# Comparison numbers in PSUM, spreads in three banks beside 45 downs, and paired heads in the mixer

## What is computed

```python
# first block, two layers: neighbourhood attention of 256 latents over themselves and 256 context
# keys (8 heads of 64), and in the first layer attention of the context over itself
s = einsum('q,k', q, k) * 64 ** -0.5 + bias
p = softmax(s);  o = p @ v

# second block: retrieval of 16 x 8 experts of 16384 for each token
q = (h @ w_q).reshape(B, TB, 8, 2, 128)
s = einsum('btphd,phnd->btphn', q, subkeys)
v, i = top_k(s, 16)
cand = v[..., 0, :, None] + v[..., 1, None, :]          # 256 candidates of a token and head
cidx = i[..., 0, :, None] * 128 + i[..., 1, None, :]
tv, tj = top_k(cand, 16);  eidx = take_along_axis(cidx, tj);  w = softmax(tv)
a = gelu(einsum('btd,btpkd->btpk', h, w_down[eidx]))
out = einsum('btpk,btpkd->btd', w * a, w_up[eidx])
```

## Time and profile before

| what | us |
|---|---|
| median of 3 runs | 3045.37 |
| lowest, highest | 3043.37, 3047.05 |
| profiled execution, device time | 3047.02 |
| its span from first to last instruction | 3045.2 |
| busy: PE, PEld | 2862.2 (94%), 2391.7 (79%) |
| busy: DVE, ACT, POOL | 2171.0 (71%), 1225.8 (40%), 534.0 (18%) |
| mixer's scores to pooled products, layer 0 | 562.9 to 644.6 |
| the same, layer 1 | 1549.4 to 1602.5 |
| downs of the retrieval | from about 2146 |
| first product of `Experts` on PE | 2415.4 |

### The profile page before, as it was taken

How to read it: one execution, slowest core, us unless ns; L and a number is a source line. 1 busy time by engine, 2 the same in 40 slices (tenths; PEclk the granted TensorE clock), 3 DMA queues, 4 the chain that set the end, 5 groups by cost and what they waited for, 6 DMA issues and landing times. The chain is left out here.

```text
span 3045.2 us, 40386 instructions
## 1 busy us (share of the span) xinstructions
PE 2862.2 (94%) x15682; PEld 2391.7 (79%) x15682; DVE 2171.0 (71%) x3813; ACT 1225.8 (40%) x2228; POOL 534.0 (18%) x403
## 2 busy tenths in 40 slices
PE   7999999999999999999899999389977899999997
PEld 4888878568888778888859999259967788888886
DVE  2999994558998975657656665446997777777776
ACT  2322243453222342223445455245544444444444
POOL 1111115000111110001400000003899600000000
PEclk9999999999999999999999999689999999999999
DMA  6445542123545454444414555304633356555553
GB/s 237 179 174 193 187 151 90 49 92 137 180 176 197 152 191 163 156 147 160 144 42 140 185 188 168 114 1 140 189 107 100 97 189 192 193 190 189 195 190 118
DMA packets 121295, 463.05 MB, mean 152 GB/s; under 512 B 13456, under 2 KB 26128, under 8 KB 107792
## 3 DMA queue, kind: packets, MB, share of 16 engines
q1 hardware_dynamic: 107280, 359.79, 35.9%
q0 software_dynamic: 13824, 100.67, 8.5%
HBM read 453.20 MB, written 7.21 MB: 151 GB/s over the span
## 5 line engine op out<-in xcount | busy, mean ns | idle before, releaser
L174 ACT ACTIVATE weight_hi<-weight_ring 128x512 fp32r<-128x512 f32 x1272 | 798.6, 631 | 1197.5 <-PE bank L264 1196.0
L181 DVE TENSOR_TENSOR weight_lo<-weight_ring,weight_hi 128x512 fp32r<-128x512 f32 x1154 | 868.7, 756 | 466.8 <-ACT weight_hi L174 465.1
L262 PE MATMUL bank<-operand_hi,weight_hi 128*128 128x256 f32 (+1 forms) x3168 | 1046.7, 330 | 28.5 <-DVE operand_lo L601 13.0
L263 PE MATMUL bank<-operand_lo,weight_hi 128*128 128x256 f32 (+1 forms) x3168 | 1036.8, 327 | 0.0
L264 PE MATMUL bank<-operand_hi,weight_lo 128*128 128x256 f32 (+1 forms) x3168 | 1036.1, 327 | 0.0
L262 PEld LDWEIGHTS bank<-operand_hi,weight_hi 128*128 128x128 f32 x3168 | 606.2, 191 | 95.7 <-issue 21.4
L263 PEld LDWEIGHTS bank<-operand_lo,weight_hi 128*128 128x128 f32 x3168 | 606.3, 191 | 52.7
L264 PEld LDWEIGHTS bank<-operand_hi,weight_lo 128*128 128x128 f32 x3168 | 606.0, 191 | 50.4
L859 DVE SCALAR_TENSOR_TENSOR extension_ffn<-extension_ffn,silu_c 128x512 f32<-128x512 f32 x532 | 388.0, 776 | 1.7
L262 PE MATMUL bank<-hidden_hi_ffn,weight_hi 128*128 128x512 f32 (+1 forms) x704 | 256.6, 364 | 4.0 <-DVE arena L1104 4.0
L263 PE MATMUL bank<-hidden_lo_ffn,weight_hi 128*128 128x512 f32 (+1 forms) x704 | 255.3, 363 | 0.0
(11 more groups left out here) (259 smaller groups left out, 2807.6 us busy)
## 6 DMA issues: line engine op xcount, KB each, us to landing
weight_ring<-in_ffn SPq DMA_DIRECT2D x272, 512.0 KB, 3.5
weight_ring<-in_experts SPq DMA_DIRECT2D x256, 512.0 KB, 3.5
extension_ffn<-in_w_mods POOLq DMA_DIRECT2D x96, 1024.0 KB, 7.6
weight_ring<-in_w_mix SPq DMA_DIRECT2D x56, 512.0 KB, 3.4
weight_ring<-in_w_second SPq DMA_DIRECT2D x52, 512.0 KB, 4.0
spill<-early_retrieve SPq DMA_DIRECT2D x47, 128.0 KB, 3.8
arena<-spill SPq DMA_DIRECT2D x47, 128.0 KB, 3.5
extension_mixer<-in_rel_bias SPq DMA_DIRECT2D x2, 1536.0 KB, 6.7
```

Of the source, the lines that this page charges most:

```text
L174: nc.scalar.activation(self.hi[:, g % 2, h], self.ring[:, g % NS, h], ACT.Copy).then_inc(self.rounded, 1)
L181: self.nc.vector.tensor_tensor(self.lo[:, g % 2, h], self.ring[:, g % NS, h], self.hi[:, g % 2, h].bitcast(F32), ALU.subtract).then_inc(se ...
L262: nc.tensor.matmul(out, a_hi, b_hi, start=start and n == 0, stop=False)
L263: nc.tensor.matmul(out, a_hi, b_lo, start=False, stop=False)
```

## The change

**The numbers of the comparison.** ACT copies `iota` (128x128) from SBUF into PSUM bank 7 once, among the query units. The 64 comparisons (now L2189) and the 4 large comparisons of `decode` (now L2247) read it there. Spreads therefore go round three banks, 4 to 6, and a spread waits for the copy of the batch three before it, not four.

**Counts.** K0 goes from 47 to 45 and ALONE from 22 to 20, so that the spreads begin two downs earlier and two more downs stand in `Experts`. HAND_OVER follows (43). `pairs` of the second half is cut in two parts of four heads, and `weights` of the first half stands between them.

**The mixer.** Items run by pairs of heads: for a tile of queries the even head, then the odd one. Scores of both heads are issued in a row, into two of four banks (0, 1, 6, 7), four items ahead and more. The values of a pair (four items) go into one bank, 64 partitions for each head, in four parts of one tile of keys for both heads; one part follows each transposition of a later item. ACT moves a pair's product in one instruction of 128 partitions, and `pt` is twice as large.

```diff
@@
-A_POOL = A_PT + 2048
+A_POOL = A_PT + 4096
@@
-        self.items = [(g, h, qt) for g in range(ng) for h in range(NA_H) for qt in range(2)]
+        self.items = [(g, 2 * hp + j, qt) for g in range(ng) for hp in range(NA_H // 2) for qt in range(2) for j in range(2)]
@@
+    def score_bank(self, w):
+        return (0, 1, 6, 7)[w % 4]
+
+    def turned_probs(self, n, j, kt):
+
+        return self.pt[:, 4 * (n % 2) + kt, :].rearrange("p (j q) -> p j q", j=2)[:, j, :]
@@
-        def scores(w):
-            g, h, qt = items[w]
-            lo, hi = keys(g)
-            po, q0 = 64 * (h % 2), g * S + qt * P
-            if w >= 2:
-                pe.wait_ge(self.scores_read.sem, self.scores_read.at(w - 1))
-            nc.tensor.matmul(chip.bank[w % 2][:, 0:hi - lo], u[po:po + 64, CH_Q + h // 2, q0:q0 + P],
-                             u[po:po + 64, CH_K + h // 2, lo:hi], start=True, stop=True)\
-                .then_inc(self.scored.sem, 1)
+        def scores(n):
+            if n >= 2:
+                pe.wait_ge(self.scores_read.sem, self.scores_read.at(2 * n - 2))
+            for w in (2 * n, 2 * n + 1):
+                g, h, qt = items[w]
+                lo, hi = keys(g)
+                po, q0 = 64 * (h % 2), g * S + qt * P
+                nc.tensor.matmul(chip.bank[self.score_bank(w)][:, 0:hi - lo], u[po:po + 64, CH_Q + h // 2, q0:q0 + P],
+                                 u[po:po + 64, CH_K + h // 2, lo:hi], start=True, stop=True)\
+                    .then_inc(self.scored.sem, 1)
@@
+            if part == 0:
+                pe.wait_ge(self.copied.sem, self.copied.at(4 * n + 4))
+                if n >= 2:
+                    pe.wait_ge(self.moved.sem, self.moved.at(n - 1))
+            for j in range(2):
+                h = items[4 * n + j][1]
+                mm = nc.tensor.matmul(chip.bank[4 + n % 2][64 * j:64 * j + 64, 0:S],
+                                      v[:, part + 4 - nkt, h * DH:(h + 1) * DH], self.turned_probs(n, j, part),
+                                      start=(part == 0), stop=(part == nkt - 1))
@@
         for w in range(len(items)):
-            if w + 3 < len(items):
-                scores(w + 3)
+            if w % 2 == 0 and w // 2 + 2 < len(items) // 2:
+                scores(w // 2 + 2)
             transposes(w)
-            if w >= 2 and w % 2 == 0:
-                values(w // 2 - 1)
-        values(len(items) // 2 - 1)
+            if w >= 4:
+                values(w // 4 - 1, w % 4)
+        for part in range(4):
+            values(len(items) // 4 - 1, part)
@@
-NQ, K0 = 16, 47
-ALONE, PAUSE = 22, 2
+NQ, K0 = 16, 45
+ALONE, PAUSE = 20, 2
@@
+        self.iota = chip.bank[7][:, 0:P]
@@
-            if b >= 4:
-                pe.wait_ge(self.kept.sem, self.kept.at(b - 3))
+            if b >= 3:
+                pe.wait_ge(self.kept.sem, self.kept.at(b - 2))
@@
+            if n == 6:
+                act.wait_ge(self.table.sem, self.table.at(17))
+                nc.scalar.activation(self.iota, chip.iota[:, :], ACT.Copy).then_inc(self.table.sem, 1)
@@
-            nc.vector.tensor_tensor(self.hots(b), iota[:, :].unsqueeze(1).unsqueeze(1).to_broadcast([P, BATCH, 2, P]),
+            nc.vector.tensor_tensor(self.hots(b), iota.unsqueeze(1).unsqueeze(1).to_broadcast([P, BATCH, 2, P]),
@@
-        pairs(1)
+        pairs(1, 0, PH // 2)
         weights(0)
+        pairs(1, PH // 2, PH)
```

More of the change, by code:

```diff
@@ L1218, in __init__ @@
             s.take(n) for s in (chip.scored, chip.scores_read, chip.maxed, chip.exped, chip.probs, chip.turned, chip.copied))
-        self.product, self.moved, self.mixed = chip.product.take(n // 2 + 1), chip.moved.take(n // 2), chip.mixed.take(1)
+        self.product, self.moved, self.mixed = chip.product.take(n // 4 + 1), chip.moved.take(n // 4), chip.mixed.take(1)
         self.y_there = chip.y_there.take(2)
@@ L1288, in transposes, with values @@
             mm.then_inc(self.turned.sem, 1)
-        def values(n):
-            g, h, _ = items[2 * n]
-            po = 64 * (h % 2)
-            pe.wait_ge(self.copied.sem, self.copied.at(2 * n + 2))
-            if n >= 2:
-                pe.wait_ge(self.moved.sem, self.moved.at(n - 1))
-            nkt = (keys(g)[1] - keys(g)[0]) // P
-            for kt in range(nkt):
-                mm = nc.tensor.matmul(chip.bank[4 + n % 2][po:po + 64, 0:S],
-                                      v[:, kt + 4 - nkt, h * DH:(h + 1) * DH], pt[:, n % 2, kt, :],
-                                      start=(kt == 0), stop=(kt == nkt - 1))
-            mm.then_inc(self.product.sem, 1)
+        def values(n, part):
+            g, _, _ = items[4 * n]
+            nkt = (keys(g)[1] - keys(g)[0]) // P
+            if part >= nkt:
+                return
+            if part == 0:
[7 more added lines that the diff above has]
+                                      start=(part == 0), stop=(part == nkt - 1))
+            if part == nkt - 1:
+                mm.then_inc(self.product.sem, 1)
         pe.wait_ge(evicted.sem, evicted.at(16))
-        for w in range(3):
-            scores(w)
+        scores(0)
         pe.wait_ge(evicted.sem, evicted.at(20))
+        scores(1)
         for w in range(len(items)):
-            if w + 3 < len(items):
-                scores(w + 3)
+            if w % 2 == 0 and w // 2 + 2 < len(items) // 2:
+                scores(w // 2 + 2)
             transposes(w)
-            if w >= 2 and w % 2 == 0:
-                values(w // 2 - 1)
-        values(len(items) // 2 - 1)
+            if w >= 4:
+                values(w // 4 - 1, w % 4)
+        for part in range(4):
+            values(len(items) // 4 - 1, part)
         pe.wait_ge(self.mixed.sem, self.mixed.at(1))
@@ L1354, in scalar @@
             copies(w)
-            if w >= 3 and w % 2 == 1:
-                move(w // 2 - 1)
-        move(len(items) // 2 - 1)
-        act.wait_ge(self.product.sem, self.product.at(len(items) // 2 + 1))
+            if w >= 8 and w % 4 == 1:
+                move(w // 4 - 2)
+        move(len(items) // 4 - 2)
+        move(len(items) // 4 - 1)
+        act.wait_ge(self.product.sem, self.product.at(len(items) // 4 + 1))
         for b in range(2):
@@ L2082, in keep @@
             nc.scalar.activation(self.weight[:, BATCH * b:BATCH * (b + 1), :].rearrange("p a b -> p (a b)"),
-                                 chip.bank[4 + b % 4][:, :], ACT.Copy).then_inc(self.kept.sem, 1)
+                                 chip.bank[4 + b % 3][:, :], ACT.Copy).then_inc(self.kept.sem, 1)
         def exp(tt):
@@ L2161, in vector @@
         cand = chip.part(E_CAND, 2, PH, TOPK * TOPK)
[L2162 removed]
+        iota16, iota = self.iota[:, 0:TOPK], self.iota
         done = [0]
@@ L2201, in best, with pairs @@
                 dve.wait_ge(chip.dve_step.sem, chip.dve_step.base)
-        def pairs(tt):
-            step(nc.vector.tensor_copy(ixf[:, tt, :, :], ix[:, tt, :, :]))
+        def pairs(tt, first, last_h):
+            if first == 0:
+                step(nc.vector.tensor_copy(ixf[:, tt, :, :], ix[:, tt, :, :]))
             vp = v[:, tt, :, :].rearrange("p (h two) k -> p h two k", two=2)
-            for h in range(PH):
+            for h in range(first, last_h):
                 last = nc.vector.tensor_tensor(
```

23 lines of the change are left out of this document (11 added, 12 removed).

## The result

The changed kernel takes 2948.8 us in the median (2947.0 to 2951.2) against 3044.5 (four runs of each; the three of before that the table ahead of the prediction used gave 3045.4): a ratio of 0.9685, 95% interval 0.9673 to 0.9696. The profiled execution took 2947.0, its span is 2945.2, 100.0 less than before. The forecast was 71 off the span, 2974 us, with a range from 2955 to 3003. The sign and the freed lock held; the mixer gained in another way than forecast, and the gain as a whole was larger than the range allowed.

What follows compares the result with a forecast made beforehand. The prediction took PE, busy 94% of 3045.2 us, as the bound, with gains only where it waits or works beyond need. Retrieval 51 plus mixer 20 made 71 off the span: median 2974 us, range 2955 to 3003.

Steps and rivals of the forecast that it cites:

- second decoding: Retrieval, DVE's later decoding: slower than PE, two halves lose 9, comparisons done ahead give part back: 5 us of slack.
- The wait at the turn: Retrieval, after 20 downs alone: PE waits 5.8 us for the first half's weights, before it was 4.0.
- the one at the first spread: Retrieval, behind the turn and half a down: PE waits 5.4 us for pairs, search, comparison and weighing.
- POOL late, 3 off: Retrieval: POOL's pace of 2.23 us leaves little room against PE's 2.33, so the gain was cut from 54 to 51.
- POOL becomes the bound: Rival, retrieval: POOL has 0.1 of room, remaining locks show at once; gain 35 instead of 51, 2990 us; chance 0.14.
- three slots for four: Mixer: two-record matmuls overlap only partly across halves; four-record scores 1.98 become 1.5, values 1.9 become 1.45 us.
- The first two heads of each layer are cold: Mixer: these heads are set by the chain through all engines, so only 14 large and 8 small heads gain.
- the last pair's values, minus 3: Mixer's end: values behind the last transposition cost 1.9 us more in layer 0 and 1 each: minus 3.
- The branch without overlap: Rival, mixer: array halves do not overlap, mixer gain 10 us, total 2984 us; chance 0.13.
- Nothing freed: Rival, retrieval: the bank operand does not end the DVE-POOL waiting; retrieval +2, mixer -20, 3027 us; chance 0.06.
- Slower by the clock: Rival, mixer: less PE work drops the granted clock to 0.50 and it stays; 3079 us; chance 0.02.
- The full overlap: Rival, mixer: halves overlap wholly, scores and values take half, mixer gain 30 us, total 2964 us; chance 0.10.

Runs made afterwards that it cites:

- index_in_bank: The changed kernel with the converted indices of the decoding moved into PSUM bank 7 beside the numbers: 2947.1 us.
- bank_and_pool: The changed kernel with converted indices in bank 7 and the mixer's division moved from DVE to POOL: 2940.6 us.
- halves_apart: The changed kernel with neighbouring mixer matmuls, scores and values, no longer on different array halves: 2975.3 us.

## Why the prediction was right or wrong

**The lock: right, in kind and size.** All 64 comparisons took the least of the earlier trace rows as assumed, most weighings 1.03 to 1.07 (seven at the end 1.42, two 3.0), spreads stand 2.33 apart outside the second decoding. The Trainium skill ("SBUF — State Buffer", "SBUF: two separate sides") has the rule that VectorE holds the shared ports when it has two SBUF inputs; here it agrees: 1.21 with one operand in a bank, a median of 2.05 with both in SBUF, in the same program but for that operand.

**The retrieval's sum: 51 forecast, 56.5 measured, inside 35 to 60**, and right by terms that offset each other. The slack left is 206.9 - (45 x 2.88 + 64 x 0.89) = 20.3 where 23 was forecast. Item by item:
- The first decoding: PE came 0.1 late to the turn (2 forecast).
- The wait at the turn 4.6 (5.8 forecast), the one at the first spread 1.0 (5.4 forecast). That second term was the failed one: `pairs` took 2.50 ahead of the weights and 1.42 behind them, not 4.05 twice, because PE and so POOL stood still and DVE was alone for most of it; and the turn with the half down behind it took PE 3.4 us, not 2.0. The price of `pairs` from the earlier trace rows held the lock's waits in it, which I had not taken out.
- The second decoding: two waits of 2.9 and 1.8, 4.7 in all (5 forecast). The reason given, that DVE is slower there than PE, holds: comparisons 3.46 apart against 2.33. What the forecast didn't know is that the lead was eaten by a shift held up for 4.4 us, without which the waits are 0.9 to 3.4; that the size came out right is partly luck. Two weighings of 3.0, held by the product L2252, stand right ahead of the two waits, but without them index_in_bank waited 5.3.
- The clock: 0.91 in three stretches of 20 us each (2165 to 2185, 2205 to 2245), 5.4 us; 2 forecast. This is the item that was short. In index_in_bank and bank_and_pool it cost nothing.
- The tail: 1.2 and 0.2 of waits (3 forecast). The items make 17.2; the other 3.1 are in none of them, 0.7 of it a wait just ahead of `Experts`.
- "POOL late, 3 off": it wasn't. The rival that POOL becomes the bound (2990) fell; in the stretch with one spread behind each half PE ran at its own pace but for the second decoding.

**The mixer: 20 forecast, 38.3 measured in the traces, 36 and 38 by medians, outside 10 to 30.** Here the prediction failed, in two steps.
- "Only the second of one head can run beside the first of the other: three slots for four." Four records take 1.13, as two did. This was a guess on issue order and no row stood behind it; the loads of the earlier trace rows overlapped wholly and were the nearer row. The Trainium skill ("TensorEngine Tiling (Array Packing)", "Key Properties"), by which tiles multiply independently, gave the right branch, and the trace agrees. That step cost 10 us; the price of a head, 5.74 to DVE's 3.96 and 3.50 to 2.5, then is what the earlier trace rows give: 3.95, and 2.2 to 2.6 for a small one.
- "The first two heads of each layer are cold", and "the last pair's values, minus 3". The distances between transpositions show that neither held. The first pairs of the two layers went from 14.1 and 13.8 us to 8.0 and 8.4, 11.5 less, where nothing was forecast; the other twelve large heads gained 18.7 and the eight small ones 8.0. (With two cold heads in each layer the prediction should also have counted 12 large heads at full gain, not 14.) The cold stretch was taken as fixed, but it moved with the order: the clock was at 0.50 from 570 to 580 before, at 0.66 for five microseconds after. And the end cost nothing: from the last transposition to the pooled product it is 1.9 us in layer 0 and 3.2 in layer 1, before and after, because eight value records of the last pair overlap too (1.08 us at 617.12). Against the bound of 30 the large heads gave 5.3 more and the end 3: the other 8 us.

The branch without overlap had 10 and came out at 11 (14 by the traces), by luck in part: a head in mid-stream gained (11.48 - 10.6) / 2 = 0.44 in halves_apart and not 0.67, a small one the 0.5 forecast, and the cold first pairs gave 8.4 that nobody had counted. So the looser order was understood in kind, and the array wasn't.

**Left out: 5.3 us** that belong to no part of the diff: 1.6 and 2.4 of clock behind the two changed stages, and 1.3 of scatter and remainder. The first is of the size of scatter between executions of the same code. The second fits what the trace of before shows at the end of the retrieval: the clock was at 0.50 from 2410 to 2419.5, across the start of `Experts` at 2415.4, and the rule used, that what stands outside the edit keeps its time, has no term for that. Whether the change ended it is not shown.

**The rivals.** "Nothing freed" was measured by putting the operand back: 3010.9 here with the better mixer. "No overlap" is halves_apart, 2975.3. "Slower by the clock" did not come: in the mixer PE's waits grew, to 0.48 in each 3.95, and the clock from 575 to 580 was still 1.00. The full overlap was right, had 0.10 and, by the loads of the earlier trace rows, deserved more; but even with it the range ended at 2955, because the cold heads and the clock were missing from its bound.

## What to carry to other kernels

Small float32 matmuls that use half of the array cost next to nothing here when the neighbour in the order used the other half (1.13 us for two, 1.12 for one), so order them by halves, and then look which engine is the floor, since it no longer is PE. Where DVE and POOL both work in SBUF, moving one operand of DVE's instruction into an unused corner of a bank frees POOL at once; then look in the trace for every other instruction of DVE that is longer beside POOL than alone, those with one operand too, since such a one can hold up what the first one freed. Take prices for a sum from stretches without the collision that the change removes, and use distances between starts, not busy times, where PE is close to another engine's pace.

## What the hardware showed that was not expected

- Float32 matmuls of two records overlap wholly across halves: 1.13 us for two of 64x512 against 1.12 for one, and 0.65 against 1.08 for four value records.
- DVE's instructions on SBUF alone wait for POOL even when they are short, the cast and the shift with one input: 1.41 us for a 128x128 subtraction that takes 0.28 elsewhere, 1.37 for a cast of 0.28, and 4.4 for a shift of 0.22 in nine of the fourteen kernels with the numbers in the bank, through POOL's instructions from 2201.91 to 2206.42 in the changed one. Their lengths depend on whether PE keeps POOL busy, so idle time of PE speeds DVE up.
- The granted clock behind a stage with waits varied between executions of the same code: in the 80 us behind the changed mixer of layer 0 it was 1.00 in three kernels and 0.98 in the others, 1.6 us. What decides it, no run here tells.
